# A two-layer hybrid decoder trunk on one core: output stored in half rows, squares summed in three parts, and tile 1's weights of the seven-product stage split in another order

## The chip, the core and the metric

The kernel runs on one core of a Trainium2 chip. Its engines have their own instruction streams and wait for one another by semaphores: TensorE (PE in the profile; PEld is its weight load) multiplies matrices, VectorE (DVE), ScalarE (ACT) and GpSimd (POOL) work on elements, SyncE (SP) issues the DMA transfers of this kernel. The metric is the device time of one execution in microseconds; lower is better.

## The reference, cut to what matters

The model has two layers over 1024 tokens of width 1024. Each layer mixes four head groups and then applies a gated feed-forward block of hidden width 2816; a last RMSNorm gives the output:

```python
u = rmsnorm(h, ln2_g[l])
h = h + (jax.nn.silu(u @ w_ffn_gate[l]) * (u @ w_ffn_up[l])) @ w_ffn_down[l]
...
return rmsnorm(h, final_norm_g)
```

All of it is float32. The change touches the gate and up products of the feed-forward block, in both layers, and the last RMSNorm.

## The kernel before

Activations are kept transposed: `h` is [128 features, 8 tiles, 1024 tokens]. Every float32 operand is split into a high part, rounded to a narrower format (fp32r in the profile), and a low part, what is left; a product is three matmuls (high x high, high x low, low x high). ACT copies the high part (`act_weight`, L2071 of the kernel before), POOL subtracts the low part (`pool_weight`, L2081).

The gate and up products of a layer are made in 22 tiles of 128 hidden features. A tile's 1024 x 256 weights are seen as a 2 x 2 block matrix (A11, A12 of the gate weights, A21, A22 of the up weights), the normed activations as another (B11 to B22, split by tokens and features), and the 2 x 2 block product is made with seven block products P1 to P7 in place of eight. For this DVE forms four weight sums S1 to S4 for each tile (`dve_sums`, L2059) and, once for each layer, four activation differences T1 to T4 (T3's low part is made at L2601). P7 is S3 x T3, P5 is S1 x T1, P6 is S2 x T2, P3 is S4 x B22, P2 is A12 x B21, P4 is A22 x T4, P1 is A11 x B11. PE takes the products of tile 1 and later in the order P1, P7, P5, P6, P2, P3, P4, each of 12 matmuls (L2120).

The order of the work is written out by hand for each engine. ACT and POOL split a tile's seven weights in the order `W_ORDER` (`W_ORDER0` for tile 0), and PE waits for a weight by its place in that order, which `weight_at` counts. The raw weights sit in one buffer for each of gate and up; SP loads tile i into it (`load_weights`, L2014) when the parts of tile i-1 that are split straight from the raw buffer and the four sums of tile i-1 are done. `act_p5` copies P5's PSUM bank, which P3 needs; in tile 1 it stands behind the copy of tile 2's A11 in ACT's stream. `dve_w` (L2157) makes the addition that P4 needs; it stands behind tile 2's sums in DVE's stream.

At the end of the last layer ACT squares the eight tiles of `h` (L279) and scales them by the norm's gain (L281), POOL adds the squares up (L291), and PE turns tiles of 128 x 128 back to token order by transposes (L2390) into eight PSUM banks, first four feature tiles of all tokens, then the other four. Sums of the squares over features, one column for each block of 128 tokens, are made by PE with a vector of ones (L2402, L2404) into the first column places of one of these banks. ACT turns them into the scale of a token (L2545, L2548), and ACT and DVE copy the banks, scaled, into `out_tokens` (L2554, L2661). SP stores 128 whole rows of 1024 at a time (L2300).

Of the kernel before, what the change touches and what calls it, by code (L numbers as in the profile page):

```python
# [35 lines left out]
P = 128  # L36
# [3 lines left out]
KT = D // P  # L40
TT = S // P
HALF = 512
# [38 lines left out]
def build(nc, x, positions, vec_table, w_in, w_uq, w_ukv, w_a, w_x, lb_logits, lam, w_out,  # L81
# [6 lines left out]
    with ctx:  # L88
# [1738 lines left out]
        W_ORDER0 = ["A11", "A12", "S1", "S2", "S4", "S3", "A22"]  # L1827
        S_ORDER = ["S3", "S1", "S2", "S4"]
# [44 lines left out]

        def weight_at(i, name):
            return 7 * i + tile_order(i, W_ORDER0, W_ORDER).index(name) + 1

# [39 lines left out]
        OUT_ORDER = [4, 5, 6, 7, 0, 1, 2, 3]  # L1916
# [77 lines left out]
        def output_ffn(l):  # L1994
# [12 lines left out]
            def load_weights(sp, i, t):  # L2007
                if i == 0:
                    sp.wait_ge(slot_split, KT - 3 + t)
                elif t == 0:  # L2010
                    sp.wait_ge(w_lo, 7 * i if i == 1 else 7 * (i - 1) + 4)
                    sp.wait_ge(s_ready, 4 * i)
                src = (w_gate, w_up)[t]
                sp.dma_start(raw[t][:, :].rearrange("p (k c) -> p k c", c=P),  # L2014
                             src[bass.ds(l * D, D), bass.ds(i * P, P)].rearrange("(k p) c -> p k c", p=P))\
                    .then_inc(raw_loaded[t], 16)
# [226 lines left out]
            def sp_part(sp):  # L2243
# [53 lines left out]
                if last_layer:  # L2297
                    for n, t in enumerate(OUT_ORDER):
                        sp.wait_ge((out_act, out_dve)[n % 2], TT // 2 + n // 2 + 1)
                        sp.dma_start(out[t * P:(t + 1) * P, :], OT[:, t, :]).then_inc(stored, 16)  # L2300
                    sp.wait_ge(stored, 16 * TT)
                else:
                    sp.wait_ge(slot_split, KT - 2 + 1)
                    load_third_slot(sp, (l + 1) * D)
                    for m in range(KT):
                        sp.wait_ge(down_added[down_pair(m)], down_used(CHUNKS - 1, m) + 1)
                        sp.dma_start(h_rows[m], h[:, m, :]).then_inc(h_moved, 16)
                    sp.wait_ge(h_moved, 16 * KT)

            def pool_part(pool):  # L2310
# [13 lines left out]
                for i in range(1, TILES):  # L2324
                    for name in W_ORDER:
                        pool_weight(pool, i, name)
# [16 lines left out]
                for m in range(KT - 1 if last_layer else KT):  # L2343
                    norm_pool(pool, norm3, m, SQ3, ACC3)
# [4 lines left out]
            def pe_part(pe):  # L2349
# [44 lines left out]
                if last_layer:  # L2394
                    pe.wait_ge(norm3[2], 4)
# [3 lines left out]
                    pe.wait_ge(norm3[1], KT - 2)  # L2399
                    pe.wait_ge(norm3[0], KT)  # L2400
                    for t in range(TT):
                        nc.tensor.matmul(ps[:, OUT_ORDER[-1], t:t + 1], ACC3[:, t * P:(t + 1) * P], ones[:, 0:1],  # L2402
                                         start=True, stop=False)
                        last = nc.tensor.matmul(ps[:, OUT_ORDER[-1], t:t + 1], SQ3[1][:, t * P:(t + 1) * P],  # L2404
                                                ones[:, 0:1], start=False, stop=True)
                    last.then_inc(ms_done, 1)
# [25 lines left out]
            def act_part(act):  # L2432
# [58 lines left out]
                for name in W_ORDER0[5:7]:  # L2491
                    act_weight(act, 0, name)
                for k in range(4):
                    u_part("T3", k)
# [7 lines left out]
                act_weight(act, 1, W_ORDER[0])  # L2502
# [4 lines left out]
                act_weight(act, 1, W_ORDER[1])  # L2507
                act.wait_ge(h_spilled, 16 * KT)
                act.wait_ge(u_dve, U_DVE_AT["T4", 3])
                for name in W_ORDER[2:]:  # L2510
                    act_weight(act, 1, name)
# [269 lines left out]
```

## Time and profile before

| | |
|---|---|
| time, median of 3 runs | 2494.59 us (2494.44 to 2495.43) |
| the profiled execution's own time | 2492.76 us |
| its span, first to last instruction | 2491.0 us, 32071 instructions |
| mean granted TensorE clock | 0.998 of full speed |
| PE, DVE, POOL, ACT busy | 2451.7, 1640.6, 956.3, 914.1 us |
| DMA | 193.23 MB, 78 GB/s over the span |
| chain that ended last, by engine | PE 92%, DVE 4%, ACT 2% |

The profile shows one execution of the program. Times in it count from the span's first instruction; the profiled time is the span and 1.76 us around it. A row of the timeline is a run of like operations: where it starts, how long it lasts, and in brackets how long its engine stood idle before it and what ended that.

### The profile page before, as it was taken

The page shows a single profiled execution, that of the slowest core. Times are in us where ns is not written, and L with a number is a line of the kernel's source. Part 1 is how long each engine was busy: PE and PEld are TensorE (multiplying, and loading weights), DVE is VectorE, ACT ScalarE, POOL GpSimd, SP SyncE. Part 2 cuts the span into 40 slices and gives each one's busy share as a digit, 9 for nine tenths or more (in the row PEclk, how much of TensorE's full clock was granted, in tenths as well). Part 3 has the DMA queues.
Part 4 walks back from the last instruction along what each step waited for, and adds up shares of the span by engine and source line. Part 5 has one row for each costly group of instructions (what it writes and reads, how often), then busy time and mean ns, then how long its engine had stood idle before and what let it go on. Part 6 is the DMA issues. An engine that isn't in the chain of part 4 may idle for free.

```text
span 2491.0 us, 32071 instructions
## 1 busy us (share of the span) xinstructions
PE 2451.7 (98%) x12772; PEld 1967.6 (79%) x12772; DVE 1640.6 (66%) x1786; ACT 914.1 (37%) x1339; POOL 956.3 (38%) x531
## 2 busy tenths in 40 slices
PE   8999999999999999999999999999999999999998
PEld 6787776787888888888877787667878888888886
DVE  7987367559665666655668953955786566655554
ACT  5444146635333333100234432765353333321003
POOL 2001412236655556433520023023565555545432
PEclk9999999999999999999999999999999999999999
DMA  5111110042222222522320211002322222243221
GB/s 195 26 44 35 41 24 2 27 144 77 93 85 81 88 76 87 193 102 102 108 64 22 48 35 43 5 1 102 101 86 85 81 89 77 85 147 138 96 102 68
DMA packets 208294, 193.23 MB, mean 78 GB/s; under 512 B 31249, under 2 KB 180881, under 8 KB 208146
## 3 DMA queue, kind: packets, MB, share of 16 engines
q1 hardware_dynamic: 208146, 191.17, 23.6%
q8 instruction: 103, 1.69, 0.3%
q14 instruction: 45, 0.37, 0.0%
HBM read 147.10 MB, written 44.04 MB: 77 GB/s over the span
## 4 chain that ended last, share of the span: by engine, by line
PE 92%; DVE 4%; ACT 2%; issue 1%; POOL 0%; DMA 0%; POOLq 0%; SPq 0%; DVEq 0%; ACTq 0%
PE ps L242 42%; PE ps L2120 31%; PE ps L1536 3%; PE ps L1513 3%; PE ps L1525 2%; PE ps L757 2%; PE ps L1984 2%; PE ps L1494 1%; PE ps L580 1%; DVE u_t L2601 1%; PE ps L1572 0%; PE ps L1241 0%; PE ps L569 0%; PE ps L2390 0%; DVE u_lo L298 0%
## 5 line engine op out<-in xcount | busy, mean ns | idle before, releaser
L2239 DVE TENSOR_TENSOR h<-ps,h 128x1024 f32<-128x1024 f32 x176 | 214.7, 1223 | 195.8 <-PE ps L242 195.0
L2081 POOL TENSOR_TENSOR w_a<-w_raw,w_a 128x512 fp32r<-128x512 f32 x110 | 178.3, 1630 | 314.5 <-ACT w_a L2071 314.5
L242 PE MATMUL ps<-u_hi,w_hi 128*128 128x512 f32 x832 | 267.1, 402 | 1.2 <-DVE h L2239 1.2
L242 PE MATMUL ps<-u_lo,w_hi 128*128 128x512 f32 x832 | 257.0, 390 | 0.0
L242 PE MATMUL ps<-u_hi,w_lo 128*128 128x512 f32 x832 | 256.8, 390 | 0.0
L2120 PE MATMUL ps<-u_b,w_a 128*128 128x512 f32 x1056 | 253.7, 390 | 0.0
L2120 PE MATMUL ps<-u_t,w_s 128*128 128x512 f32 x1056 | 247.5, 390 | 4.1 <-POOL w_s L2081 4.1
L2120 PEld LDWEIGHTS ps<-u_t,w_s 128*128 128x128 f32 x1056 | 198.0, 188 | 46.5 <-POOL w_s L2081 5.6
L2120 PEld LDWEIGHTS ps<-u_b,w_a 128*128 128x128 f32 x1056 | 198.4, 188 | 40.9
L242 PE MATMUL ps<-hidden_lo,down_hi 128*128 128x512 f32 x640 | 197.4, 390 | 0.0
L242 PE MATMUL ps<-hidden_hi,down_hi 128*128 128x512 f32 x640 | 197.3, 390 | 0.0
L242 PE MATMUL ps<-hidden_hi,down_lo 128*128 128x512 f32 x640 | 197.2, 390 | 0.0
L242 PEld LDWEIGHTS ps<-u_hi,w_hi 128*128 128x128 f32 x832 | 153.8, 188 | 39.2 <-issue 8.1
L242 PEld LDWEIGHTS ps<-u_lo,w_hi 128*128 128x128 f32 x832 | 156.3, 188 | 32.9
L242 PEld LDWEIGHTS ps<-u_hi,w_lo 128*128 128x128 f32 x832 | 156.3, 188 | 32.9
L2209 ACT ACTIVATE hidden_hi<-hidden_back 128x1024 fp32r<-128x1024 f32 x44 | 44.9, 1055 | 353.5 <-PE ps L242 304.3
L2195 POOL TENSOR_TENSOR down_hi<-w_raw,ones 128x1024 fp32r<-128x1024 f32 x40 | 77.8, 1945 | 248.7 <-PE ps L242 204.3
L2081 POOL TENSOR_TENSOR w_s<-w_s_raw,w_s 128x512 fp32r<-128x512 f32 x110 | 164.0, 1506 | 14.7 <-ACT w_s L2071 14.7
L226 POOL TENSOR_TENSOR w_hi<-w_raw,ones 128x1024 fp32r<-128x1024 f32 (+1 forms) x25 | 46.1, 1844 | 321.1 <-issue 180.6
L2120 PE MATMUL ps<-u_t,w_hi 128*128 128x512 f32 x528 | 163.8, 392 | 2.6 <-DVE u_t L2601 2.6
L2144 ACT ACTIVATE hidden_gate<-hidden_gate 128x1024 f32<-128x1024 f32 x44 | 46.7, 1062 | 261.9 <-DVE hidden_gate L2172 261.9
L242 PEld LDWEIGHTS ps<-hidden_lo,down_hi 128*128 128x128 f32 x640 | 120.2, 188 | 25.0
(388 smaller groups left out, 4899.4 us busy)
## 6 DMA issues: line engine op xcount, KB each, us to landing
w_raw<-w_gate SPq DMA_DIRECT2D x44, 512.0 KB, 3.7
w_raw<-w_up SPq DMA_DIRECT2D x44, 512.0 KB, 4.8
hidden_spill<-hidden_gate SPq DMA_DIRECT2D x44, 512.0 KB, 2.6
w_raw<-w_down SPq DMA_DIRECT2D x44, 512.0 KB, 4.5
hidden_back<-hidden_spill SPq DMA_DIRECT2D x44, 512.0 KB, 4.1
w_raw<-w_in SPq DMA_DIRECT2D x42, 512.0 KB, 3.8
h_spill<-h SPq DMA_DIRECT2D x32, 512.0 KB, 4.4
h<-h_spill SPq DMA_DIRECT2D x32, 512.0 KB, 7.8
```

What stands on the lines that cost most here:

```text
L226: nc.gpsimd.tensor_tensor(hi[:, 0:width], raw[i][:, 0:width], ones[:, 0:1].broadcast_to([P, width]), ALU.mult).then_inc(hi_split, 1)
L242: last = nc.tensor.matmul(ps[:, bank0 + half, :], a, b[:, half * HALF:(half + 1) * HALF], start=(k == order[0] and n == 0), stop=(k == ord ...
L757: last = nc.tensor.matmul(ps[0:keys, 4 + 2 * (L % 2) + j, c * 64:(c + 1) * 64], KL[L % 2][rows, c * P:c * P + keys], QL[L % 2][rows, c, :] ...
L1513: nc.tensor.matmul(ps[:, 2 * j + a // HALF, 0:e - a], QH[p][0:96, j, q_at], KH[p][0:96, j, a:e], start=True, stop=True)
L1525: last = nc.tensor.transpose(ps[:, unit_bank(u), (b - b0) * P:(b - b0 + 1) * P], src[:, b * P:(b + 1) * P], ident)
L1536: last = nc.tensor.matmul(ps[head_rows(j), 7, 0:P], v[:, i % PAIRS, b, head_rows(j)], pt[j][:, b, :], start=(b == 0), stop=(b == keys - 1))
L1984: last = nc.tensor.matmul(ps[:, 2 * (j % 4) + half, :], a, b[:, half * HALF:(half + 1) * HALF], start=(k == MIX_ORDER[0] and n == 0), stop ...
L2081: nc.gpsimd.tensor_tensor(lo, src, hi.bitcast(F32), ALU.subtract).then_inc(w_lo, 1)
L2120: last = nc.tensor.matmul(ps[:, bank(i, name), :], x, y, start=new and k == 0 and n == 0, stop=k == 3 and n == 2, skip_group_check=True)
L2144: nc.scalar.activation(GA[:, :], GA[:, :], ACT.Silu).then_inc(silu_done, 1)
L2195: nc.gpsimd.tensor_tensor(hi[t][:, :], DRAW[t][:, :], ones[:, 0:1].broadcast_to([P, D]), ALU.mult).then_inc(down_hi, 1)
L2239: nc.vector.tensor_tensor(wide(h[:, m, :]), pair(p), wide(h[:, m, :]), ALU.add)\
```

## The change

There are four edits.

1. The output is stored in halves of rows: 16 stores of 128 x 512 in place of 8 of 128 x 1024, the first half of all token blocks first. The order of token blocks is 4, 5, 6, 0, 1, 2, 3, 7 in place of 4, 5, 6, 7, 0, 1, 2, 3.
2. The sums of squares are made in three parts (POOL's running sum of six squares, the seventh square, the eighth), each by eight matmuls, ahead of all transposes. POOL adds one square less.
3. Tile 1's weights have an order of their own, in which S1 and S2 stand ahead of A22; the load of the next tile waits for the last of A11, A12, A22 in whatever order the tile has.
4. In ACT's stream the first two high parts of T3 stand ahead of the high parts of tile 0's S3 and A22.

```diff
+        W_ORDER1 = ["A11", "S3", "A12", "S1", "S2", "A22", "S4"]
...
+        def weight_order(i):
+            return W_ORDER1 if i == 1 else tile_order(i, W_ORDER0, W_ORDER)
+
         def weight_at(i, name):
-            return 7 * i + tile_order(i, W_ORDER0, W_ORDER).index(name) + 1
+            return 7 * i + weight_order(i).index(name) + 1
...
-        OUT_ORDER = [4, 5, 6, 7, 0, 1, 2, 3]
+        OUT_ORDER = [4, 5, 6, 0, 1, 2, 3, 7]
...
-                    sp.wait_ge(w_lo, 7 * i if i == 1 else 7 * (i - 1) + 4)
+                    sp.wait_ge(w_lo, max(weight_at(i - 1, a) for a in ("A11", "A12", "A22")))
                     sp.wait_ge(s_ready, 4 * i)
...
-                    for n, t in enumerate(OUT_ORDER):
-                        sp.wait_ge((out_act, out_dve)[n % 2], TT // 2 + n // 2 + 1)
-                        sp.dma_start(out[t * P:(t + 1) * P, :], OT[:, t, :]).then_inc(stored, 16)
-                    sp.wait_ge(stored, 16 * TT)
+                    for part in range(2):
+                        at = slice(part * HALF, (part + 1) * HALF)
+                        for n, t in enumerate(OUT_ORDER):
+                            sp.wait_ge((out_act, out_dve)[n % 2], TT // 2 * part + n // 2 + 1)
+                            sp.dma_start(out[t * P:(t + 1) * P, at], OT[:, t, at]).then_inc(stored, 16)
+                    sp.wait_ge(stored, 32 * TT)
...
-                for m in range(KT - 1 if last_layer else KT):
+                for m in range(KT - 2 if last_layer else KT):
                     norm_pool(pool, norm3, m, SQ3, ACC3)
...
+                    def token_sums(squares, first, end):
+                        for t in range(TT):
+                            last = nc.tensor.matmul(ps[:, OUT_ORDER[-1], t:t + 1], squares[:, t * P:(t + 1) * P],
+                                                    ones[:, 0:1], start=first and t == 0, stop=end,
+                                                    skip_group_check=True)
+                        return last
+
+                    pe.wait_ge(down_added[OUT_ORDER[-1] // 2], 2 * CHUNKS)
+                    pe.wait_ge(norm3[1], KT - 3)
+                    token_sums(ACC3, True, False)
+                    pe.wait_ge(norm3[0], KT - 1)
+                    token_sums(SQ3[0], False, False)
+                    pe.wait_ge(norm3[0], KT)
+                    token_sums(SQ3[1], False, True).then_inc(ms_done, 1)
                     pe.wait_ge(norm3[2], 4)
                     for t in OUT_ORDER[:-1]:
                         pe.wait_ge(down_added[t // 2], 2 * CHUNKS)
                         to_tokens(t, 0)
-                    pe.wait_ge(norm3[1], KT - 2)
-                    pe.wait_ge(norm3[0], KT)
-                    for t in range(TT):
...
-                for name in W_ORDER0[5:7]:
-                    act_weight(act, 0, name)
-                for k in range(4):
+                u_part("T3", 0)
+                act_weight(act, 0, W_ORDER0[5])
+                u_part("T3", 1)
+                act_weight(act, 0, W_ORDER0[6])
+                for k in range(2, 4):
                     u_part("T3", k)
```

What the edits move is seen best in the order of the instructions. On POOL, the low parts of tile 1's seven weights (names that begin with w1) in the kernel before, and behind them the first of tile 2:

```order
75 L2081 TENSOR_TENSOR w1_a11_182<-w_raw0_64,w1_a11_182 128x512
76 L2081 TENSOR_TENSOR w1_s3_184<-w1_s3_raw_185,w1_s3_184 128x512
77 L2081 TENSOR_TENSOR w1_a12_190<-w_raw0_64,w1_a12_190 128x512
78 L2081 TENSOR_TENSOR w1_a22_194<-w_raw1_65,w1_a22_194 128x512
79 L2081 TENSOR_TENSOR w1_s1_186<-w1_s1_raw_187,w1_s1_186 128x512
80 L2081 TENSOR_TENSOR w1_s2_188<-w1_s2_raw_189,w1_s2_188 128x512
81 L2081 TENSOR_TENSOR w1_s4_192<-w1_s4_raw_193,w1_s4_192 128x512
82 L2081 TENSOR_TENSOR w0_a11_176<-w_raw0_64,w0_a11_176 128x512
```

The same place in the changed kernel:

```order
75 L2085 TENSOR_TENSOR w1_a11_182<-w_raw0_64,w1_a11_182 128x512
76 L2085 TENSOR_TENSOR w1_s3_184<-w1_s3_raw_185,w1_s3_184 128x512
77 L2085 TENSOR_TENSOR w1_a12_190<-w_raw0_64,w1_a12_190 128x512
78 L2085 TENSOR_TENSOR w1_s1_186<-w1_s1_raw_187,w1_s1_186 128x512
79 L2085 TENSOR_TENSOR w1_s2_188<-w1_s2_raw_189,w1_s2_188 128x512
80 L2085 TENSOR_TENSOR w1_a22_194<-w_raw1_65,w1_a22_194 128x512
81 L2085 TENSOR_TENSOR w1_s4_192<-w1_s4_raw_193,w1_s4_192 128x512
82 L2085 TENSOR_TENSOR w0_a11_176<-w_raw0_64,w0_a11_176 128x512
```

S1 and S2 have moved up by one place, and A22, the last of the three that read the raw buffers (w_raw0, w_raw1), from the fourth place to the sixth.

On ACT, from the last square of tile 0's norm (sq2) to the two bank copies, in the kernel before; w_hi1 holds the high parts of S3 and then A22, u_t3 those of T3:

```order
323 L2450 ACTIVATE u_b21_200<-h_77,vectors_52 128x512
324 L279 ACTIVATE sq2_1_172<-h_77 128x1024
325 L2071 ACTIVATE w_hi1_67<-w_sum1_175 128x512
326 L2071 ACTIVATE w_hi1_67<-w_raw1_65 128x512
327 L2458 ACTIVATE u_t3_206<-h_77 128x512 x4
328 L2128 ACTIVATE p1_copy_210<-ps 128x512
```

And in the changed kernel:

```order
324 L279 ACTIVATE sq2_1_172<-h_77 128x1024
325 L2470 ACTIVATE u_t3_206<-h_77 128x512
326 L2075 ACTIVATE w_hi1_67<-w_sum1_175 128x512
327 L2470 ACTIVATE u_t3_206<-h_77 128x512
328 L2075 ACTIVATE w_hi1_67<-w_raw1_65 128x512
329 L2470 ACTIVATE u_t3_206<-h_77 128x512 x2
330 L2132 ACTIVATE p1_copy_210<-ps 128x512
```

T3's first part stands ahead of S3, the second between S3 and A22; the bank copies stay behind all of them.

On PE, the end of the program in the kernel before: the last four transposes ahead of the sums, and the first of the sums, which take POOL's running sum (acc) and the last square (sq) in turn:

```order
4624 L2390 MATMUL ps<-constants,final_scaled_233 128x128
4625 L2390 MATMUL ps<-constants,final_scaled_234 128x128
4626 L2390 MATMUL ps<-constants,final_scaled_235 128x128
4627 L2390 MATMUL ps<-constants,final_scaled_236 128x128
4628 L2402 MATMUL ps<-ones,acc_232 128x1
4629 L2404 MATMUL ps<-ones,sq_1_231 128x1
```

In the changed kernel, with the last product of the down projection ahead:

```order
4598 L242 MATMUL ps<-hidden_lo_228,down_hi_221 128x512 x2
4599 L242 MATMUL ps<-hidden_hi_226,down_lo_223 128x512 x2
4600 L2403 MATMUL ps<-ones,acc_232 128x1 x8
4601 L2403 MATMUL ps<-ones,sq_0_230 128x1 x8
4602 L2403 MATMUL ps<-ones,sq_1_231 128x1 x8
4603 L2396 MATMUL ps<-constants,final_scaled_233 128x128
4604 L2396 MATMUL ps<-constants,final_scaled_234 128x128
4605 L2396 MATMUL ps<-constants,final_scaled_235 128x128
```

The 24 sums now follow the last product at once, and all 64 transposes follow the sums.

## Rows read from the trace of the kernel before

**Rows 1.** Chain of waits, 600 to 640 us: start, us, what

```profile
622.53 383.99 PE ps L2120 x1692
```

**Rows 2.** What PE waited for, whole span: us in total, times, longest

```profile
PE ps L2120 <- POOL w_s L2081: 4.1, 2, 2.1
PE ps L2120 <- DVE u_t L2601: 2.6, 2, 1.3
```

**Rows 3.** Timeline of ACT: start us, us, engine, line, operation, tiles, [idle before <-releaser]

```profile
615.32 0.63 ACT L2071 ACTIVATE w_a<-w_raw 128x512 fp32r<-128x512 f32 x1 [1.58 <-issue]
615.86 0.58 ACT L2134 ACTIVATE p_copy<-ps 128x512 f32<-128x512 f32 x1
```

**Rows 4.** Timeline of DVE, 586 to 622 us

```profile
586.46 5.96 DVE L2601 TENSOR_TENSOR u_t<-h,u_t 128x512 fp32r<-128x512 f32 x4 [1.08 <-ACT u_t L2458]
608.29 1.66 DVE L2059 TENSOR_TENSOR w_s_raw<-w_raw,w_s_raw 128x512 f32<-128x512 f32 x1
616.56 1.77 DVE L2059 TENSOR_TENSOR w_sum<-w_raw,w_raw 128x512 f32<-128x512 f32 x1
618.26 0.68 DVE L2059 TENSOR_TENSOR w_s_raw<-w_raw 128x512 f32<-128x512 f32 x1
621.67 0.69 DVE L2157 TENSOR_TENSOR w_sum<-ps,v_copy 128x512 f32<-128x512 f32 x1 [0.31 <-ACT v_copy L2140]
```

**Rows 5.** Timeline of POOL, S1 and S2 of tile 1

```profile
609.36 1.72 POOL L2081 TENSOR_TENSOR w_s<-w_s_raw,w_s 128x512 fp32r<-128x512 f32 x1
611.04 2.27 POOL L2081 TENSOR_TENSOR w_s<-w_s_raw,w_s 128x512 fp32r<-128x512 f32 x1
```

**Rows 6.** Timeline of PE, tile 1: P5 and P6, P3, P4

```profile
611.14 5.73 PE L2120 MATMUL ps<-u_t,w_s 128*128 128x512 f32 x24 [2.07 <-POOL w_s L2081]
619.43 2.88 PE L2120 MATMUL ps<-u_b,w_s 128*128 128x512 f32 x12
622.51 2.97 PE L2120 MATMUL ps<-u_t,w_a 128*128 128x512 f32 x12 [0.20 <-POOL w_a L2081]
```

**Rows 7.** Timeline of SP, first load of tile 2

```profile
610.03 0.37 SPq L2014 DMA_DIRECT2D w_raw<-w_gate  x1
```

**Rows 8.** Timelines of POOL, PE, ACT, DVE and SP, the tail

```profile
2464.51 2.41 POOL L291 TENSOR_TENSOR acc<-acc,sq 128x1024 f32<-128x1024 f32 x1
2466.94 3.22 PE L2390 MATMUL ps<-constants,final_scaled 128*128 128x128 f32 x28
2473.66 0.27 ACT L2545 ACTIVATE final_rs<-ps,eps 128x8 f32<-128x8 f32 x1 [3.17 <-PE ps L2404]
2474.20 2.48 DVE L2661 TENSOR_TENSOR out_tokens<-ps,final_rs 128x512 f32<-128x512 f32 x4 [5.84 <-ACT final_rs L2548]
2477.23 8.00 SPq L2300 DMA_DIRECT2D out<-out_tokens  x8
```

**Rows 9.** Busy time by stretch; the third number from the end is the granted clock

```profile
2470.00:2473.60 3.60, 3.60 (x34) 3.54 (x32) 0.00 (x0) 0.50 (x1) 0.00 (x0) 1.00 0.00 0
2474.00:2477.00 3.00, 3.00 (x14) 2.69 (x15) 2.48 (x4) 2.97 (x6) 0.00 (x0) 0.50 0.00 0
2477.50:2478.50 1.00, 1.00 (x11) 1.00 (x10) 0.55 (x2) 0.69 (x1) 0.00 (x0) 1.00 0.43 180
```

**Rows 10.** DMA view, GB/s in 40 slices: 2476 to 2490, then 610 to 616 us

```profile
GB/s 0 0 0 47 0 82 386 410 363 211 281 421 410 398 457 410 421 375 480 410 421 375 480 398 421 386 456 410 421 398 456 410 421 398 456 141 23 0 0 0
GB/s 0 0 0 0 0 0 0 126 109 113 61 222 259 331 345 338 341 358 345 345 345 341 341 358 345 348 348 348 338 290 181 96 17 0 0 0 0 0 0 0
```

**Rows 11.** Instructions of lines L2300 and L2020: issue ns min/median/max, us to landing

```profile
L2300 SPq DMA_DIRECT2D out<-out_tokens x8: 337/1151/1418, 2477.2 to 2484.0; - x8
DMA to landing us min/median/max: 3.5/5.0/5.3
...
L2020 SPq DMA_DIRECT2D hidden_spill<-hidden_gate x44: 326/339/476, 616.7 to 2235.4; - x44
DMA to landing us min/median/max: 2.6/2.6/14.1
```

More of the change, by code:

```diff
@@ L2324, in pool_part @@
                 for i in range(1, TILES):
-                    for name in W_ORDER:
+                    for name in weight_order(i):
                         pool_weight(pool, i, name)
@@ L2398, in pe_part @@
                         to_tokens(t, 0)
-                    pe.wait_ge(norm3[1], KT - 2)
-                    pe.wait_ge(norm3[0], KT)
-                    for t in range(TT):
[L2402 to L2406, printed above, removed]
                     pe.wait_ge(rs_part, 2)
@@ L2501, in act_part @@
                 act.wait_ge(proj_done, J_OUT + KT + 1)
-                act_weight(act, 1, W_ORDER[0])
+                act_weight(act, 1, W_ORDER1[0])
                 norm_rs(act, 0, (rs_part, 1))
@@ L2506, in act_part @@
                     u_part("T4", k)
-                act_weight(act, 1, W_ORDER[1])
+                act_weight(act, 1, W_ORDER1[1])
                 act.wait_ge(h_spilled, 16 * KT)
                 act.wait_ge(u_dve, U_DVE_AT["T4", 3])
-                for name in W_ORDER[2:]:
+                for name in W_ORDER1[2:]:
                     act_weight(act, 1, name)
```

## Prediction

> **What bounds the kernel now.** I read the busy line, where TensorE (PE) fills nearly the whole span, then the list of what PE waited for, then timelines around those waits, and the DMA view of the end. In the seven-product stage of a layer nothing but PE counts once it runs: from 622.53 us it issues 1692 matmuls without a pause [rows 1], so whatever delays it before that moves the rest of the program as one piece. The edits sit at three places where PE does wait or where it ends: tile 0's P7, which waits for T3's low part (1.3 us in each layer), tile 1's P5, which waits for S1's low part (2.1 us in each layer) [rows 2], and the tail, where the stores end last. Both layers look alike; I work with the first and double it.
>
> **T3 moved up.** Before it splits T3, VectorE (DVE) sits idle 1.08 us until 586.46, for ScalarE (ACT) copies S3 and A22 ahead of T3's first high part [rows 4]. S3's copy waits for a sum of DVE anyway, so I cost T3's part ahead of it at nothing; were it 0.5 late, P7 asks for S3 only some 3 us later. DVE can then start at about 585.3. But its four subtractions need 5.96 us where a free one of that width takes 0.68 (the sum at 618.26, 1.70 after 616.56, is free) [rows 4]: DVE and GpSimd (POOL) take turns, each ending its operation only after the other's. POOL's three operations there (S3, A22 and a full-row addition) now each let one subtraction pass ahead, and the addition ends about 0.4 us later; the fourth subtraction follows it at about 592.2 against 592.4. PE's wait goes from T3's third quarter to its fourth. P7 gains 0.25 us; of this 0.2 arrives at tile 1, since T2, B22 and T4 behind it on ACT and DVE gain that much too. Bounds 0 (POOL's S3 takes its turn first, as now) and 1.3 (the wait gone); I take 0.2, since the turns are what the rows show.
>
> **S1 before A22.** POOL's S1 now runs 609.36 to 611.08 [rows 5], behind A22, and P5 starts at 611.14 [rows 6]. In the new order it waits for the sum S2, which ends at 608.26 (S4's sum starts behind it at 608.29 [rows 4]), at 608.05 with the gain above. DVE's S4 sum follows within 0.03 us and I let it go first (0.68): 608.75. POOL ended 1.13 us after DVE released it (609.95 to 611.08), so S1 is done at 609.9 and P5 starts at 609.95, 1.2 us earlier. If POOL wins the turn, 1.7.
>
> **What is late next: the loads of tile 2.** They are queued on SyncE (SP) behind the low parts of A11, A12 and A22 and behind tile 1's sums. Before, A22 was the fourth low part and the last wait was for the S4 sum: 608.29 + 1.66 = 609.95, first load issued at 610.03 [rows 4, 7]. Now A22 is sixth, behind S1 and S2, and these two and A22 run beside DVE's full-row multiplications of tile 0, where one took POOL 2.27 us [rows 5]: S2 ends at 609.9 + 2.25 = 612.15, A22 at 614.4. The loads go out 4.4 us later, at 614.45. Before, 5.29 us passed from the first load's issue to ACT's A11 of tile 2 (610.03 to 615.32) [rows 3, 7]; so A11 is copied at 619.75.
> On ACT the copy of P5's bank is queued behind that A11: 0.54 us later, as now (615.32, 615.86 [rows 3]), done at 620.85. PE's P3 needs it. Before, P3 started at 619.43, 8.29 behind P5 [rows 6]; now it could at 618.25 and does at 620.9.
> On DVE tile 2's four sums wait for the same loads, and the addition (w_sum) that P4 needs is queued behind them and behind ACT's V copy. Before, the first sum was entered at 616.56 and the addition at 621.67; P4 started at 622.51 [rows 4, 6]. Now the first sum starts at 619.75 and meets an idle POOL (0.68), the second 0.60 later likewise, the third and fourth take turns with POOL's A11 and S3 (about 1.7 each, as 1.66 at 608.29): 619.75 + 0.60 + 0.68 + 1.69 + 1.72 = 624.45, the addition ends at 625.1, P4 starts at 625.2, 2.7 us late. P1 of tile 2 follows, its A11 ready; tile 3's loads come some 3 us later, tile 3's consumers do too, and PE has no further wait. So 2.7 us are lost in each layer, all gains above counted; with POOL winning the turn at S1, everything from A22 on is 0.9 earlier and 1.8 are lost. I take 2.6: the turn is DVE's in my reading. Bounds: with no turns at all A22 ends at 612.0 and 1.3 are gained; with loads 1.4 us slower than the one at 610.03, 4.1 are lost. Two layers: **+5.2 us**.
>
> **The tail.** Before: last product, 28 transposes from 2466.94, 16 sums of squares, the root from 2473.66, the first scaled copy at 2474.20, the first whole-row store at 2477.23 [rows 8]. PE's sums now come first. POOL's addition of the sixth square ends at 2464.51 + 2.41 = 2466.92, just with the last product, so leaving the seventh to PE lets the sums start 3 us earlier. They are 24 for 16: 16 took 3.65 us (2470.0 to 2473.65), so 24 take 5.45, to 2472.4. Root 0.54 with the first tile's four transposes beside it (28 in 3.22 us: 0.46), copy 0.69: first half-row store at 2473.7, 3.5 us earlier. That is at the full clock. The granted clock was 1.00 through the 16 sums, 0.50 (1.2 GHz) from 2474 to 2477 and 1.00 again [rows 9]. With 24 sums the fall can come inside them. As a bound I let it come eight sums before the last; these take at most twice as long (+1.8), and four transposes 0.86 (14 in 3.00 us): first store 2475.8, 1.4 earlier, and then tiles come every 0.86 us where a half row needs 0.62 of transfer, some 0.9 lost less the 0.5 that the old stream lost at its start.
> After the start the stream sets the end: 4.19 MB moved at 400 to 430 GB/s between 2478 and 2488.4 [rows 10]. Rows of 2 KB are not in the trace as a stream; 512-byte loads ran at 345 [rows 10], which would cost 2 us, 4 KB rows cost nothing; nearer to these, 0.3. Eight more issues: one unhindered takes 0.34 us, the 1.15 of the old stores is one transfer's time, a full queue [rows 11]; 0.62 of transfer covers 0.34 to 0.48. So the end comes 3.2 to 0.7 us earlier (or 1.0 later with both bad ends); I take **-2.0**, the middle, for the trace shows the clock's fall once only and not where it lands now.
>
> A page would have it otherwise. The Trainium skill (TensorE: Matmul & The Clock Gate, Part 4) says that the full clock does not engage for transposes. By it the half clock would last through all 64 of them, and the end would come 3.0 us later than in my sum, as the third rival works out from rows. The rows differ: nothing but transposes ran from 2474, and the clock was back by 2477.5 [rows 9]; I follow the rows and leave the rule a small chance.
>
> **Sum.** +5.2 - 2.0 = +3.2 on the profiled 2492.76 (span 2491.0 and 1.76 around it): 2496.0. The median of the runs lies 1.83 above the profiled one: **2497.8**, 0.13% slower, inside the 0.2% (5.0 us) that a measurement of this kernel can tell from no change.
>
> **Rivals.**
> 1. The loads come in time. If turns are lost less often than I think, A22 ends by 612.0 and P3 and P4 find their inputs: 1.3 gained in each layer, -2.6 - 2.0 = -4.6; with a tail at its best -5.8: 2489 to 2490. For it: P3 had 3 us of room after its copy (616.44 to 619.43). Against: the rows show a turn at every POOL operation of that stretch.
> 2. Slower: SP issues become the bound of the tail. If each of 16 stores kept 1.15 us, they would take 18.4 us from 2473.7, and the last lands at about 2494 against 2489: +5, with the layers +10: 2505. It decides from 0.8 us for an issue on. Against it: 0.34 [rows 11].
> 3. Slower: the half clock lasts to the end. 64 transposes at 0.214 are 13.7 us from 2473.5, last copy 2487.9; its store lands 2.0 later (2.6 for 512 KB alone, less half the transfer [rows 11]), at 2489.9 against 2489.0 (2484.0 + 5.0 [rows 11]): +1 instead of -2.0, in all +6.2, 2501. Half of that decides already; against it stands the return in [rows 9].
> 4. The tail gains little while the layers lose 2.7 each: +5, on the border.
>
> **Chances.** The forecast, -1 to +4.9, 0.68, all within 0.2%; rival 1 0.17 (0.10 faster, 0.07 within); rival 2 0.05 and rival 3 0.04, slower; rival 4 0.06, half of it slower. Faster 0.10, same 0.78, slower 0.12. The range 2490.5 to 2500.5 leaves out a part of rival 1 and rivals 2 and 3; the likeliest case alone runs from 2493.6 to 2499.5.
>
> **What would show it.** Right: P5 of tile 1 starts about 1.2 us sooner after tile 0's P7 than before; tile 2's loads are issued some 4.5 us after it, not 1 us before it; PE then waits at P3 and P4 of tile 1, named after the copy on ACT and w_sum on DVE; T3's wait stays at 1 us or more. First store 1.4 to 3.5 us earlier against the last product, issues well under 0.62. Wrong: no wait at P3, or a stall that moves on into tile 2; a store stream with gaps behind issues.

## The result and the profile after

The changed kernel takes 2499.2 us (median of 11 runs, 2498.39 to 2501.78); the kernel before, beside it on the same chip, 2494.44 us (11 runs, 2492.95 to 2495.43). The medians differ by 4.8 us. The ratio, which the differences of the experiments below are taken from too, is 1.0023, with a 95% interval of 1.0015 to 1.0031: 5.7 us slower (3.7 to 7.7), on the border of the 0.2% (5.0 us) that the prediction named. The range (2490.5 to 2500.5) holds it; the forecast, 2497.8 us, is 1.4 us under it.

The profiled execution of the changed kernel took 2501.65 us, its span is 2499.9 us. That is 8.9 us over the span of before, more than the 4.8 of the medians, because the profiled execution of before lies 1.7 us under its median and this one 2.45 us over its own (eight of its eleven runs lie between 2498.4 and 2500.0, three between 2501.2 and 2501.8, and the profile is one of the three). So the sum of waits below adds up to the 8.9 of these two executions, not to the 4.8 or 5.7 of the runs.

What PE waited for in the changed kernel, over the whole span (us in total, times, longest), against [rows 2]:

```profile
PE ps L2124 <- ACT p_copy L2138: 6.1, 2, 3.1
PE ps L2124 <- POOL w_s L2085: 2.2, 2, 1.1
PE ps L2124 <- DVE u_t L2615: 2.0, 2, 1.0
```

S1's wait has halved, from 4.1 to 2.2 us, T3's went from 2.6 to 2.0, and a third one is new and larger than both gains: 3 us in each layer for the copy of P5's bank. A fourth, for w_sum at P4, is 1.2 us in layer 2 alone (the row at 1852.04 below); why layer 1 doesn't have it comes out of the clock. The timeline of PE in the changed kernel, tile 1 of the first layer (start, us, engine, line, operation, tiles, and in brackets the idle time before it and what ended that), against [rows 6]; the first row is P2 of tile 0, ahead of every edit:

```profile
586.66 2.88 PE L2124 MATMUL ps<-u_b,w_a 128*128 128x512 f32 x12
...
610.30 5.81 PE L2124 MATMUL ps<-u_t,w_s 128*128 128x512 f32 x24 [1.09 <-POOL w_s L2085]
615.95 2.88 PE L2124 MATMUL ps<-u_b,w_a 128*128 128x512 f32 x12
621.92 5.46 PE L2124 MATMUL ps<-u_b,w_s 128*128 128x512 f32 x12 [3.09 <-ACT p_copy L2138]
627.18 3.21 PE L2124 MATMUL ps<-u_t,w_a 128*128 128x512 f32 x12
```

Layer 2 of the same timeline: P1 of tile 0, then P5, P3 and P4 of tile 1:

```profile
1807.27 2.88 PE L2124 MATMUL ps<-u_b,w_a 128*128 128x512 f32 x12
...
1836.33 5.76 PE L2124 MATMUL ps<-u_t,w_s 128*128 128x512 f32 x24 [1.09 <-POOL w_s L2085]
...
1847.84 3.00 PE L2124 MATMUL ps<-u_b,w_s 128*128 128x512 f32 x12 [3.04 <-ACT p_copy L2138]
1852.04 2.98 PE L2124 MATMUL ps<-u_t,w_a 128*128 128x512 f32 x12 [1.20 <-DVE w_sum L2161]
```

And three rows of the kernel before that these stand against: P2 of tile 0, then in layer 2 P1 of tile 0, and P4 of tile 1:

```profile
586.29 2.88 PE L2120 MATMUL ps<-u_b,w_a 128*128 128x512 f32 x12
...
1802.34 2.88 PE L2120 MATMUL ps<-u_b,w_a 128*128 128x512 f32 x12
...
1843.95 2.98 PE L2120 MATMUL ps<-u_t,w_a 128*128 128x512 f32 x12 [0.16 <-DVE w_sum L2157]
```

This execution was 0.37 us late before the first edit (586.66 against 586.29). P5 starts at 610.30 against 611.14 [rows 6], 1.2 us earlier when the 0.37 are taken off. P4 ends at 630.39 against 625.48 [rows 6]: 4.91 late, so 4.5 are lost in the first layer. In the second layer P1 of tile 0 started at 1807.27 here, 4.93 late, and P4 ends at 1855.02 against 1846.93, 8.09 late: 3.2 are lost.

The layers differ in one row. P3 of the first layer took 5.46 us for what takes 2.88 or 3.00 elsewhere. The windows of PE there (start and end, us, PE busy with its instructions, granted clock, DMA share, GB/s):

```profile
619.00:622.00 3.00, 0.08 (x1) 0.82 0.57 214
622.00:627.20 5.20, 5.20 (x13) 0.50 0.00 0
627.20:630.00 2.80, 2.80 (x13) 0.90 0.12 30
```

The granted clock fell to 0.50, the lower level (1.2 GHz), while PE waited, and came back some 0.5 us into P4 (the mean of 0.90 from 627.20 to 630.00). Without that, P3 would have left PE at 624.64 (2.72 after its start, the step of a full-clock product), and P4 would have waited for w_sum as in layer 2: w_sum was done at 625.96 (row below), so P4 could start 0.14 later, as in layer 2, at 626.10 and end at 629.08. By this estimate the clock cost 1.3 us; 3.2 remain, as in layer 2.

Why P3 waits stands in the timelines of SP, ACT, DVE and POOL (against [rows 3 to 5] and [rows 7]). SP and ACT:

```profile
614.76 0.37 SPq L2018 DMA_DIRECT2D w_raw<-w_gate  x1
...
620.66 0.63 ACT L2075 ACTIVATE w_a<-w_raw 128x512 fp32r<-128x512 f32 x1 [7.71 <-issue]
621.20 0.58 ACT L2138 ACTIVATE p_copy<-ps 128x512 f32<-128x512 f32 x1
```

DVE, from S4's sum of tile 1 to the addition that P4 needs:

```profile
608.43 0.69 DVE L2063 TENSOR_TENSOR w_s_raw<-w_raw,w_s_raw 128x512 f32<-128x512 f32 x1
...
620.67 0.69 DVE L2063 TENSOR_TENSOR w_sum<-w_raw,w_raw 128x512 f32<-128x512 f32 x1 [4.86 <-DMA w_raw<-w_up]
...
623.70 1.66 DVE L2063 TENSOR_TENSOR w_sum<-w_raw,w_sum 128x512 f32<-128x512 f32 x1
625.28 0.68 DVE L2161 TENSOR_TENSOR w_sum<-ps,v_copy 128x512 f32<-128x512 f32 x1
```

POOL, the low parts of S1 and S2 in one row, then A22:

```profile
608.54 3.95 POOL L2085 TENSOR_TENSOR w_s<-w_s_raw,w_s 128x512 fp32r<-128x512 f32 x2 [0.70 <-DVE w_s_raw L2063]
612.45 2.28 POOL L2085 TENSOR_TENSOR w_a<-w_raw,w_a 128x512 fp32r<-128x512 f32 x1
```

The eye goes down a chain: A22 ends at 614.73, the first load of tile 2 is issued at 614.76 (610.03 before), it lets ACT's A11 run at 620.66, P5's copy stands behind that and ends at 621.78, P3 starts at 621.92. DVE's four sums wait for the same loads, and w_sum stands behind them.

At the end of the program PE, with the last product of the down projection, the 24 sums (two records for each) and the 64 transposes, and SP's 16 stores (against [rows 8]):

```profile
2474.57 0.61 PE L242 MATMUL ps<-hidden_hi,down_lo 128*128 128x512 f32 x2
2475.14 1.92 PE L2403 MATMUL ps<-ones,acc 128*128 128x1 f32 x16
2476.91 6.20 PE L2403 MATMUL ps<-ones,sq 128*128 128x1 f32 x32
2482.98 9.62 PE L2396 MATMUL ps<-constants,final_scaled 128*128 128x128 f32 x64
2484.89 10.43 SPq L2306 DMA_DIRECT2D out<-out_tokens  x16
```

The windows there (columns as before, with PEld, DVE, ACT and POOL behind PE; the granted clock is the third number from the end), against [rows 9]:

```profile
2475.00:2476.90 1.90, 1.90 (x17) 1.79 (x17) 1.23 (x1) 1.28 (x2) 0.00 (x0) 1.00 0.00 0
2476.90:2478.00 1.10, 1.10 (x11) 1.10 (x10) 0.00 (x0) 1.10 (x2) 0.00 (x0) 0.89 0.00 0
2478.00:2488.00 10.00, 10.00 (x48) 10.00 (x49) 1.38 (x2) 2.90 (x6) 0.00 (x0) 0.50 0.20 76
2488.00:2494.00 6.00, 4.60 (x42) 4.36 (x40) 4.15 (x6) 3.66 (x6) 0.00 (x0) 1.00 0.95 363
```

The clock falls in the middle of the sums and stays at 0.50 for 10 us, through the rest of the sums and the first 23 or so transposes (5 us at the 0.21 us of one, as 14 in 3.00 in [rows 9]). The sums take 7.84 us (2475.14 to 2482.98); the first store goes out 9.75 us after the first sum, where before it went out 10.29 us after the last product (2466.94 to 2477.23 [rows 8]). From the first sum to the end of the span it is 24.8 us, and from the last product 24.1 before (2491.0 - 2466.94). So the first store goes out 0.5 us sooner, and what comes behind it, from its issue to the end of the span, takes 15.0 us (2484.89 to 2499.9) against 13.8 (2477.23 to 2491.0), 1.2 longer. The stores (issue ns min, median, max, first and last start; us to landing), against [rows 11]:

```profile
L2306 SPq DMA_DIRECT2D out<-out_tokens x16: 332/458/700, 2484.9 to 2494.6; - x16
...
DMA to landing us min/median/max: 2.4/3.0/3.6
```

In this execution: 0.37 at the start, 4.5 and 3.2 in the layers, 0.7 in the tail, 8.8 of the 8.9 us.

### The profile page after: what moved, and what is told of

It is laid out like the page before. It is cut to its first block, busy times and chain, and to the rows that moved or that the text cites. A ratio compares the mean times of both kernels' runs of the same rounds, so it can differ in the third digit from the quotient of the medians.

```text
span 2499.9 us, 32109 instructions
## 1 busy us (share of the span) xinstructions
PE 2460.0 (98%) x12788; PEld 1972.7 (79%) x12788; DVE 1641.5 (66%) x1786; ACT 914.4 (37%) x1339; POOL 955.9 (38%) x530
## 4 chain that ended last, share of the span: by engine, by line
PE 92%; DVE 4%; ACT 2%; issue 1%; DMA 1%; POOL 1%; POOLq 0%; SPq 0%; DVEq 0%; ACTq 0%
PE ps L242 42%; PE ps L2124 31%; PE ps L1536 3%; PE ps L1513 3%; PE ps L1525 2%; PE ps L757 2%; PE ps L1988 2%; PE ps L1494 1%; PE ps L580 1%; DVE u_t L2615 1%; PE ps L1572 0%; PE ps L1241 0%; PE ps L2396 0%; DVE w_s_raw L2063 0%; PE ps L569 0%
## 5 line engine op out<-in xcount | busy, mean ns | idle before, releaser
L242 PEld LDWEIGHTS ps<-hidden_hi,down_lo 128*128 128x128 f32 x640 | 120.1, 188 | 25.1
```

What stands on the lines that cost most here:

```text
L242: last = nc.tensor.matmul(ps[:, bank0 + half, :], a, b[:, half * HALF:(half + 1) * HALF], start=(k == order[0] and n == 0), stop=(k == ord ...
```

## Experiments

All times are medians beside runs of the kernel before on the same chip; a difference in us is the ratio's, on 2494.

| run | edits in it | median us | before | ratio (95%) |
|---|---|---|---|---|
| e1_tail_only | 1, 2 | 2494.57 | 2493.61 | 1.0002 (0.9993 to 1.0011) |
| e2_order_only | 3 | 2500.14 | 2493.61 | 1.0026 (1.0015 to 1.0036) |
| e3_t3_only | 4 | 2493.05 | 2493.61 | 0.9998 (0.9990 to 1.0007) |
| e4_halves_only | 1 | 2493.68 | 2493.61 | 0.9996 (0.9988 to 1.0005) |
| e5_sums_only | 2 | 2497.22 | 2494.21 | 1.0014 (1.0005 to 1.0022) |
| e6_p5_first | 3, 4, P5's copy moved | 2502.63 | 2494.21 | 1.0038 (1.0024 to 1.0051) |
| e7_p5_v_w_first | and V's copy, w_sum | 2492.83 | 2494.21 | 0.9994 (0.9985 to 1.0003) |
| e8_v_w_first_halves | and 1 | 2491.53 | 2494.21 | 0.9992 (0.9984 to 1.0001) |
| e9_p5_first_twice | and P5's copy of tile 2 | 2490.09 | 2494.31 | 0.9986 (0.9977 to 0.9995) |
| e10_sums_among | and sums among transposes | 2491.19 | 2494.31 | 0.9986 (0.9977 to 0.9994) |

### Each edit by itself

Theory A is the prediction's: the order of tile 1's weights loses in the layers, through the late loads, and the rest is small. Theory B puts the loss in the tail.

The tail alone (e1): the changed kernel with both layer edits undone.

```diff
-        W_ORDER1 = ["A11", "S3", "A12", "S1", "S2", "A22", "S4"]
+        W_ORDER1 = ["A11", "S3", "A12", "A22", "S1", "S2", "S4"]
...
-                u_part("T3", 0)
-                act_weight(act, 0, W_ORDER0[5])
...
+                for name in W_ORDER0[5:7]:
+                    act_weight(act, 0, name)
+                for k in range(4):
+                    u_part("T3", k)
```

> Only the two edits of the tail (half-row stores, 24 sums ahead of the transposes). Theory A (the loss is made in the two layers, where tile 2's loads are late): 0 to -2 us against before, with the granted clock at 0.50 from about two thirds of the sums on and a first store less than 2 us earlier. Rival B (the loss is the tail's own: sums and transposes at half clock, 16 stores): +4 to +5 us, the whole loss of the change.

Measured: +0.5 us (-1.7 to +2.7). The loss is not in the tail, but neither are the 2 us that the prediction gave it.

The order alone (e2): T3's edit undone as above, stores and sums as before, only `W_ORDER1` and the loads' wait changed.

> Only tile 1's weight order, in both layers. Theory A: loads of tile 2 issued some 4.5 us later than before, PE waits about 3 us at P3 of tile 1, and the kernel is 6 us slower (3.2 in each layer), or 8 to 9 where the granted clock falls to half in that wait. Rival B (PE's late waits only use up slack that it had, the 1 us won at P5 stays): 0 to -2 us.

Measured: +6.5 us (3.7 to 9.0), the whole loss. Its profile has both waits for P5's copy, and P3 behind each at 4.6 us in place of 2.9 (first and second layer):

```profile
622.59 4.59 PE L2124 MATMUL ps<-u_b,w_s 128*128 128x512 f32 x12 [2.60 <-ACT p_copy L2138]
1847.45 4.57 PE L2124 MATMUL ps<-u_b,w_s 128*128 128x512 f32 x12 [2.95 <-ACT p_copy L2138]
```

So the clock fell in both layers, and yet the whole is 6.5 us, not the 8 to 9 that theory A had for this case. From P7 of tile 1 to P1 of tile 2 its two layers take 22.37 and 22.71 us where the kernel before takes 19.26 in each: 3.1 and 3.5 lost. w_sum was done only at 626.62 and 1851.48, and P4 started at 627.01 and 1851.86, so at the full clock P4 could have started some 0.25 us sooner in each, an estimate with 0.14 us from w_sum to P4 as above; the slow P3 cost no more than that.

T3 alone (e3): `W_ORDER1` in the old order, stores and sums as before.

> Only T3's first two high parts ahead of S3 and A22 on ACT. Theory A (DVE's four subtractions still end behind POOL's full-row addition): PE's wait in tile 0's P7 shrinks from 1.3 to about 1.0 us and moves from the third quarter to the fourth, -0.2 us in each layer, -0.4 in all, not told from no change. Rival B: the wait goes, -2.6 us.

Measured: -0.5 us (-2.5 to +1.7), and the wait for T3 is 2.0 us in both layers together, 1.0 each, in place of 2.6. The size lies under what the runs can tell; the wait shows the step.

Half rows alone (e4) and sums alone (e5) take the tail apart. In e4 the order of blocks is 4, 5, 6, 7, 0 to 3 as before, and the sums are the old 16 behind 28 transposes:

```diff
-        OUT_ORDER = [4, 5, 6, 0, 1, 2, 3, 7]
+        OUT_ORDER = [4, 5, 6, 7, 0, 1, 2, 3]
...
-                    token_sums(ACC3, True, False)
-                    pe.wait_ge(norm3[0], KT - 1)
-                    token_sums(SQ3[0], False, False)
...
+                        nc.tensor.matmul(ps[:, OUT_ORDER[-1], t:t + 1], ACC3[:, t * P:(t + 1) * P], ones[:, 0:1],
+                                         start=True, stop=False)
```

> Only the half-row stores; sums and transposes as before. Theory A (the stream of stores ends the kernel, and an issue takes 0.35 to 0.5 us where the queue isn't full): the first store 2.3 us earlier against the last product (when the first half row is scaled), the end 1.5 to 2.3 us earlier. Rival B (16 issues or rows of 2 KB make the stream longer): 0 to +3 us, DMA below 380 GB/s in the stream or issues of 0.7 us and more.

Measured: -1.0 us (-3.0 to +1.2), less than expected. In its profile the stores start 2.2 us earlier after the last product than before (2469.42 to 2477.47, 8.05 against 10.29), but the span ends only 0.9 earlier (23.2 against 24.1): the stores and what comes behind them take 15.1 us, against 13.8. The clock was at 0.50 from 2476.0 to 2482.6 here, and the 36 transposes behind the root took 7.23 us, against 5.88 in the profile of before, but this is not what holds the end. e8 and e9 below have this tail too, e8 with 5.87 us for the 36 transposes, and from the first store to the end of the span they take 15.1 and 14.9 us. The six profiles with half rows all lie between 14.9 and 15.2 there, the six with whole rows between 12.9 and 13.8. So the stream of half rows is the longer one by more than 1 us, as rival B had it, though at 0.46 us for an issue (median) and some 400 GB/s, outside the signs that it named.

e5 keeps the sums and edit 1's order of blocks and takes the half rows away (layers as before):

```diff
-                    for part in range(2):
-                        at = slice(part * HALF, (part + 1) * HALF)
...
+                    for n, t in enumerate(OUT_ORDER):
+                        sp.wait_ge((out_act, out_dve)[n % 2], TT // 2 + n // 2 + 1)
+                        sp.dma_start(out[t * P:(t + 1) * P, :], OT[:, t, :]).then_inc(stored, 16)
```

> Edit 2 alone: 24 sums ahead of all transposes, output still in eight stores of whole rows, layers as before. Theory A (the tail's loss is the clock, which falls to 0.50 inside the sums and stays there while the output starts; the half rows do no harm): 24 sums take 7 to 8 us after the last product in place of 28 transposes and 16 sums in 6.7; with whole rows the first store needs both halves of a block, so it starts later than the 10.3 us of before, about 11.5 to 12; time +1 to +3 us against before. Theory B (the sums come early enough, the loss is in the half-row stores): first store at 9 to 9.5 us, time -1 to -2 us. Layers: PE waits of before, 4.1 us for S1 and 2.6 us for T3.

Measured: +3.5 us (1.2 to 5.5), theory A and more. The timelines of PE and SP in its tail, and two windows (granted clock third from the end):

```profile
2467.31 1.92 PE L2401 MATMUL ps<-ones,acc 128*128 128x1 f32 x16
2469.08 6.34 PE L2401 MATMUL ps<-ones,sq 128*128 128x1 f32 x32
2475.28 9.49 PE L2394 MATMUL ps<-constants,final_scaled 128*128 128x128 f32 x64
2482.47 7.61 SPq L2304 DMA_DIRECT2D out<-out_tokens  x8
```

```profile
2467.00:2470.00 3.00, 3.00 (x26) 2.73 (x24) 1.22 (x1) 2.38 (x3) 0.16 (x1) 0.96 0.00 0
2470.00:2479.60 9.60, 9.60 (x47) 9.60 (x48) 1.32 (x2) 2.60 (x5) 0.00 (x0) 0.50 0.00 1
```

The first whole row needs the root and 36 transposes behind it, and all of that now runs at the half clock: 15.2 us to the first store (expected 12 at most), 28.1 to the end of the span. With e1, the tail from the last product to the end of the span has four corners, one profile each: 24.1 before, 23.2 with half rows, 28.1 with the sums ahead, 24.7 with both. So the sums ahead cost 4.0 us with whole rows and 1.5 with half rows, where the first store needs 4 transposes and not 36. Other profiles bear two of the corners out: 23.6 to 24.1 in the five with whole rows and the 16 sums (before, e2, e3, e6, e7), 23.2, 23.1 and 22.9 with half rows (e4, e8, e9).

### What holds P3 and P4

In e6 the copy of P5's bank stands ahead of tile 2's A11 on ACT; the tail is that of before, the order and T3 are changed.

```diff
+                        act_p5(act, i)
                         act_weight(act, i + 1, W_ORDER[0])
-                        act_p5(act, i)
```

> Edits 3 and 4 with the tail of before, and in tile 1 the copy of P5's bank ahead of tile 2's A11 in ACT's stream. Theory A (both the copy and w_sum are late, and w_sum is the later one, since it stands behind tile 2's four sums on DVE): P3's wait is gone, but P4 now waits for w_sum, 2.5 to 4 us in each layer, and each layer still loses 2.7 to 3.3: +5 to +6.5 us against before, hardly better than the +6.5 of the two edits without this. Theory B (the copy alone holds the path): no wait at P4 over 0.5 us, -2 to -3 us against before.

Measured: +9.5 us (6.0 to 12.7); the medians differ by 8.4. Theory A: the wait at P3 is gone, P4 waits in its stead. PE in its first layer, P3 and P4, and the window of P4:

```profile
618.50 2.88 PE L2124 MATMUL ps<-u_b,w_s 128*128 128x512 f32 x12
625.45 4.42 PE L2124 MATMUL ps<-u_t,w_a 128*128 128x512 f32 x12 [4.06 <-DVE w_sum L2161]
```

```profile
625.40:629.60 4.20, 4.15 (x12) 3.35 (x13) 4.17 (x4) 0.00 (x0) 4.20 (x4) 0.65 0.14 33
```

That it comes out slower than the order alone (8.4 us against 6.5 by the medians) was expected by neither theory, though the two intervals overlap. P4 starts when w_sum allows, as it would in e2, but the time that PE stands idle is now one piece of 4.1 us (5.0 in layer 2), and P4 behind it runs mostly at the half clock (4.42 and 4.58 us for 2.88).

e7 goes on: V's copy goes ahead of tile 2's A11 on ACT, and w_sum ahead of tile 2's sums on DVE.

```diff
                         act_p5(act, i)
+                        act_v(act, i)
                         act_weight(act, i + 1, W_ORDER[0])
...
+                    if i == 1:
+                        dve_w(dve, i)
                     if i + 1 < TILES:
                         dve_sums(dve, i + 1, S_ORDER)
-                    dve_w(dve, i)
+                    if i > 1:
+                        dve_w(dve, i)
```

> As the run before, and in tile 1 the copy of V ahead of tile 2's A11 on ACT and w_sum ahead of tile 2's sums on DVE, so that nothing of tile 1's P3 and P4 stands behind the loads of tile 2. Theory A (the late loads cost only through these two queues): no wait at P3 and P4, P5's 1.2 us per layer arrive at tile 2, T3's 0.2 to 0.3 too: -2.4 to -3.2 us against before. Theory B (late loads stall tile 2 itself, for its weights are split late): a new wait for w_a or w_s at tile 2's P1 or P7, 1 us or more in each layer, time within 1 us of before or slower.

Measured: -1.5 us (-3.7 to +0.7), between the two theories, and its trace has something of both. P3, P4 and P1 of tile 2 follow one another without a wait, as theory A had it; but a new wait does come, not for a weight at P1 or P7, as theory B had it, but at P3 of tile 2, for the same copy one tile on:

```profile
617.63 2.88 PE L2124 MATMUL ps<-u_b,w_s 128*128 128x512 f32 x12
620.35 2.88 PE L2124 MATMUL ps<-u_t,w_a 128*128 128x512 f32 x12
623.07 2.88 PE L2124 MATMUL ps<-u_b,w_a 128*128 128x512 f32 x12
...
637.56 0.70 PE L2124 MATMUL ps<-u_b,w_hi 128*128 128x512 f32 x2 [0.74 <-ACT p_copy L2138]
```

Tile 3's loads were issued at 626.75, and in tile 2 P5's copy stands behind four of tile 3's high parts. Layer 2 has the same wait with 1.04 us. Of the 1.2 us gained at P5 in each layer, 0.74 and 1.04 were given back there.

e8 is e7 with the half-row stores and the 16 sums; the order of blocks is the old one (4, 5, 6, 7, 0 to 3), not edit 1's, which the expectation names.

> The run before with the half-row stores of edit 1 and its order of blocks, sums in 16 as before, among the transposes. Theory A (half rows gain about 1 us in the tail when the clock does not fall early): -3 to -4.5 us against before, faster than both kernels. Theory B (the half rows gain nothing, as in the median of their run alone, -0.8 with an interval that reaches past zero): as the run before, -2.4 to -3.2.

Measured: -2.0 us (-4.0 to +0.2), by the medians -2.7. The number is near theory B's, but e7 itself had measured less than was expected of it, and e8's median is 1.3 us under e7's, with intervals that overlap. The times tell the two theories apart no better than e4 did; the tails do (23.1 us against 24.0 in e7, from the last product to the end of the span).

e9 takes e8 and puts P5's copy of tile 2, too, ahead of the next tile's weights.

```diff
-                    if i == 1:
+                    if i <= 2:
                         act_p5(act, i)
+                    if i == 1:
                         act_v(act, i)
...
+                    if i > 2:
+                        act_p5(act, i)
```

> The run with the V copy, w_sum and half rows, and in tile 2, too, the copy of P5's bank ahead of the next tile's weights on ACT. Theory A (tile 3's loads are late as well, and cost only through this copy, for which tile 2's P3 waited 0.7 and 1.0 us): that wait goes and nothing takes its place, -1.7 us against the run without this, so about 2489.8 us, -4.4 us against before. Theory B (the stall moves on, to w_sum at tile 2's P4 or to tile 3): a new wait of 0.7 us or more in each layer, time within 0.5 us of the run without this, about 2491.5.

Measured: 2490.09 us, -3.5 us (-5.7 to -1.2); by the medians -4.2, and 1.4 less than e8. Theory A: no wait for p_copy or w_sum of 0.1 us or more is left in PE's list, and nothing took their place but 0.2 us, once, for a low part (w_a). This version beats both kernels.

### The clock in the tail

e10 mixes e9's 16 sums with the last eight of the 28 transposes.

```diff
+                        block, k = OUT_ORDER[-3 + t // 4], t % 4
+                        turned = nc.tensor.transpose(ps[:, block, k * P:(k + 1) * P],
+                                                     HG[k][:, block * P:(block + 1) * P], ident)
```

> As the run before, and the 16 sums of squares mixed with eight of the 28 transposes, one transpose behind each pair of sums, in place of all 16 behind the 28. The instructions are the same. Theory A (the clock falls because one-column matmuls stand in a row): the granted clock is not 0.50 in the 3 to 7 us behind the sums, or for a shorter time; the 36 transposes behind the root take under 5 us in place of 5.9 to 7.2, and the time is 0.5 to 1.5 us lower. Theory B (the clock falls some 4 us after the first sum whatever stands between): same fall, time within 0.5 us.

Measured: 2491.19 us, 1.1 over e9 by the medians, with intervals that overlap. Neither theory held. Windows of its tail, the sums from 2467.55 on:

```profile
2467.50:2469.70 2.20, 2.15 (x20) 2.18 (x21) 0.00 (x0) 0.84 (x1) 0.00 (x0) 0.98 0.00 0
2469.70:2479.60 9.90, 9.86 (x48) 9.26 (x48) 3.87 (x6) 4.37 (x9) 0.00 (x0) 0.50 0.42 161
```

And of e9's, the sums, then the stretch behind the root:

```profile
2468.20:2471.60 3.40, 3.40 (x34) 3.40 (x32) 0.00 (x0) 0.48 (x1) 0.00 (x0) 1.00 0.00 0
2472.80:2476.00 3.20, 2.87 (x14) 2.80 (x14) 2.77 (x5) 2.60 (x5) 0.00 (x0) 0.50 0.67 257
2476.00:2482.00 6.00, 2.28 (x21) 2.04 (x19) 2.07 (x3) 2.06 (x3) 0.00 (x0) 1.00 1.03 395
```

With one transpose behind each pair of sums the clock fell some 2 us after the first sum, not later, and stayed low for 10 us; in e9 it fell behind the sums and was back after about 3.4 us. Its first store goes out 10.0 us after the last product, against 8.0 in e9, and the tail is 24.9 us against 22.9. PE also stood idle for 0.42 us ahead of e10's first sum, which e9 doesn't have, so the mixing is not the only difference. What sets the moment of the fall and of the return stays open.

## Why the prediction was right, and where it was not

**S1 before A22: right.** P5 was put at 609.95; with the 0.37 by which this execution is late, 610.32, and it starts at 610.30. S4's sum on DVE went ahead of POOL's S1 (608.43 against 608.54), the turn that the prediction chose.

**The loads: right in mechanism and moment.** Predicted 614.45, 614.82 with the 0.37; issued at 614.76. From there to ACT's A11 the prediction took 5.29 us of the kernel before; it was 5.90 here. Over the seven profiles with the new order it was 5.3 to 5.9 us in the first layer and 5.7 to 6.4 in the second, over the five with the old order 5.2 to 5.5 and 5.2 to 5.3. With the new order the store of tile 0's hidden values is issued 1.1 us after the first load (615.84 here; with the old order only when the loads had landed, 616.7 before); whether it is what slows them was not tested.

**P3 and P4: right in place, the size too small.** Both waits stand where they were put, named after p_copy and w_sum. Lost were 3.2 us in each layer at the full clock, where the prediction took 2.6; the longer load is nearly all of the 0.6 (ACT's A11 at 620.66, less 0.37, against 619.75). What it didn't have is the clock: by the estimate above 1.3 us more in the layer where it fell to 0.50 during the wait. The term of +5.2 measured 7.7 in the profile of the changed kernel (4.5 and 3.2), and e2 gives the order 6.5 us.

**T3: right.** The wait moved to the fourth quarter of P7 and is 1.0 us in each layer, which the prediction had as "1 us or more"; e3 is -0.5 us for 0.4 predicted.

**The tail: the step that failed.** The prediction took -2.0; the profile has +0.7 and e1 +0.5 (-1.7 to +2.7). The sums did start with the last product, but 24 took 7.84 us, not 5.45 (5.48 at the rate of 16 in 3.65), since the clock fell about 2.6 us into them. The prediction had this as a bound (+1.8 for the sums, a first store 1.4 us sooner, gain 0.7), and took the middle between it and no fall. The bound itself did not go far enough: it let the last 8 sums run slow where some 12 did, so that the first store came 0.5 us sooner, not 1.4. And it priced what comes on top behind the first store at 0.7 us (0.3 for the rows of 2 KB, 0.4 for tiles that come slowly), where the profile has 1.2 (15.0 against 13.8): 0.5 gained and 1.2 lost are the +0.7. e5 shows what the sums ahead are worth with whole rows: a loss of 3.5 us.

**The half rows: right on the issues, too cheap on the stream.** 16 issues took 0.33 to 0.70 us each, median 0.46, so rival 2 (SP as the bound, from 0.8 us on) is out. The stream of 2 KB rows, in 40 slices from 2480 to 2499 us of the changed kernel's DMA view:

```profile
GB/s 0 0 0 0 0 0 0 0 0 0 0 0 371 229 392 267 384 289 285 341 220 379 405 405 414 410 405 401 405 401 410 397 414 410 405 392 39 13 0 0
```

Its steady part, 14 slices from 405 to 392, has a mean of 405 GB/s; that of whole rows in [rows 10], 24 slices from 421 to 456, has 420. For 4.2 MB this is 0.4 us, an estimate, near the 0.3 that the prediction took for it. But with half rows all profiles take over 1 us longer from the first store to the end of the span (14.9 to 15.2 us against 12.9 to 13.8), whether the transposes ran slow or not. In the changed kernel the first 4.75 us of the stream, beside slow transposes, moved 220 to 392 GB/s; in e4, e8 and e9 the stream starts at full rate and ends with some 1.4 us at 18 to 29. What makes up the rest of the difference was not taken apart.

**The rivals.** Rival 1 (loads in time) is out by the waits. Rival 3 (half clock to the end) came halfway: 10 us of it, then the return at 2488, while nothing but transposes ran. The Trainium skill (TensorE: Matmul & The Clock Gate, Part 4) has it that the full clock does not engage for transposes. The 1.00 from 2488 to 2494, as that of [rows 9], says otherwise, though here some 23 of them ran at 0.50 first; in all twelve profiles the clock came back while nothing but transposes ran. Rival 4 (the tail gains little, +5) is what happened in the sum, with a chance of 0.06. The forecast's time was near because the layers were well placed (+5.2 against +6.0 by e2 and e3 together); its tail had the wrong sign. Both terms came out slower than forecast, so no two errors cancelled.

**The sum.** Predicted +5.2 - 2.0 = +3.2. By the ratios: order +6.5, T3 -0.5, tail +0.5, together +6.5, and the whole kernel +5.7 (3.7 to 7.7), each with an interval of 2 us or more on either side. That the parts add up is as much as these runs can say.

## What to carry to other kernels

When an operation is moved up, look for who else waited for the one that it overtook: here A22's place set the load of the next tile, and through two in-order queues two products of the tile in work. Work of the current tile (P5's copy, V's copy, w_sum) belongs ahead of work that waits for the next tile's loads; moving only the first in the queue turned one wait into a longer one (e6), and with the rest moved too the wait went to the next tile until it was moved there as well (e7, e9). Where the end of a program is a row of small matmuls, price it at both clock levels before moving it onto the path. Where stores are cut smaller to start sooner, measure the stream behind the first store too: here 2.2 us sooner at the start were 0.9 at the end (e4).

## What the runs showed of the hardware

- A wait of PE between products can cost more than its length: behind 2.6 to 5.0 us of idle PE, the product that followed ran at a granted clock of 0.50 for most of it (5.46 us in the changed kernel, 4.59 and 4.57 in e2, 4.42 and 4.58 in e6, for 2.88), but behind 3.04 us in layer 2 of the changed kernel's profile it didn't (3.00), nor behind the 2.07 us at P5 of the kernel before.
- In the tails the stretch at 0.50 lasted some 3.4 us (before, e2, e3, e6, e8, e9), 6.8 us (e4, e7) or 10 us (the changed kernel, e1, e5, e10). e3 and e7 have the same tail and differ, so the program alone doesn't set it. The clock had fallen each time between 2 and 5 us after the first of the one-column matmuls.
- Output rows of 2 KB streamed at 405 GB/s in the mean of their steady part, rows of 4 KB at 420. From the first store to the end of the span, 16 stores of 128 x 2 KB took 14.9 to 15.2 us in six profiles, 8 stores of 128 x 4 KB 12.9 to 13.8 in six others.
